# Second-layer attention of a three-layer model: probabilities divided by their sums before the transpose, values as the stationary operand

## The reference, cut to what matters

```python
qkv = h @ w_qkv + b_qkv                      # 3 x 16 heads x 64
q = qkv[0] * (NA_HEAD_DIM ** -0.5)
s = einsum('bhqd,bhkd->bhqk', qr, kb) + bias  # bias from rpb, 256 x 256 per head
s = where(key_mask, s, -inf)
a = softmax(s, axis=-1)
o = einsum('bhqk,bhkd->bhqd', a, vb)
return o @ w_o                               # (256 x 1024) @ (1024 x 1024)
```

## Time and profile before

| what | value |
|---|---|
| runs | 1015.31 us median of 3 (1015.08 to 1017.59) |
| profiled execution | 1015.26 us, span 1013.4 us |
| mean granted TensorE clock | 0.997 |
| TensorE busy | 993.4 us, 98% of the span, 5869 matmul records |
| VectorE, ScalarE, GpSimd busy | 635.6 (63%), 506.4 (50%), 129.3 us (13%) |
| chain that ended last | TensorE 91%, VectorE 5%, ScalarE 2% |
| mean DMA rate | 172 GB/s |

### The profile page before, as it was taken

The page is one execution under the profiler, slowest core; times in us unless marked ns, Lnnn a source line. Parts: engine busy times, 40 slices in busy tenths (PEclk is TensorE's granted clock), DMA queues, the critical chain, the costliest instruction groups (busy, mean ns, idle before and its releaser), DMA issues.

```text
span 1013.4 us, 14604 instructions
## 1 busy us (share of the span) xinstructions
PE 993.4 (98%) x5869; PEld 865.7 (85%) x5869; DVE 635.6 (63%) x981; ACT 506.4 (50%) x751; POOL 129.3 (13%) x207
## 2 busy tenths in 40 slices
PE   7999999999999999999999999999999999999997
PEld 6889788888888898988888888888989889999995
DVE  6867677555556875555765555568665877555554
ACT  7666745444444655554544444456564355434442
POOL 5000796800000000000000000012500000000000
PEclk9999999999999999999999999999999999999999
DMA  9944469955555564243475555545643337656521
GB/s 277 299 136 143 104 154 209 301 175 199 179 195 177 176 204 145 111 126 125 150 244 178 195 181 193 183 132 195 191 163 110 100 125 253 204 168 205 171 81 42
DMA packets 112724, 174.77 MB, mean 172 GB/s; under 512 B 5977, under 2 KB 73569, under 8 KB 112657
## 3 DMA queue, kind: packets, MB, share of 16 engines
q1 hardware_dynamic: 106224, 165.43, 51.0%
q0 software_dynamic: 6272, 8.15, 3.3%
q10 hardware_dynamic: 160, 0.27, 0.1%
HBM read 172.77 MB, written 1.05 MB: 172 GB/s over the span
## 4 chain that ended last, share of the span: by engine, by line
PE 91%; DVE 5%; ACT 2%; DMA 1%; issue 1%; SPq 0%; DVEq 0%; ACTq 0%
PE bank L1017 27%; PE bank L1019 27%; PE bank L1018 27%; PE bank L1130 2%; DVE wl L1531 1%; PE bank L1160 1%; PE bank L1032 1%; PE bank L1187 1%; DMA raw<-in_da_w_qkv_dram 1%; PE bank L1246 1%; PE bank L1193 1%; PE bank L1180 1%; PE bank L1140 1%; ACT wh L607 1%; PE bank L1163 0%
## 5 line engine op out<-in xcount | busy, mean ns | idle before, releaser
L1531 DVE TENSOR_TENSOR wl<-raw,wh 128x2048 fp32r<-128x2048 f32 x154 | 355.2, 2312 | 185.2 <-ACT wh L607 185.1
L607 ACT ACTIVATE wh<-raw 128x2048 fp32r<-128x2048 f32 x154 | 292.0, 1909 | 118.4 <-PE bank L1019 111.8
L1017 PE MATMUL bank<-wh,xh 128*128 128x512 f32 (+2 forms) x664 | 250.5, 377 | 1.6 <-DVE xl L1608 1.0
L1019 PE MATMUL bank<-wh,xl 128*128 128x512 f32 (+2 forms) x664 | 245.9, 370 | 0.0
L1018 PE MATMUL bank<-wl,xh 128*128 128x512 f32 (+2 forms) x664 | 245.8, 370 | 0.0
L1017 PE MATMUL bank<-xh,wh 128*128 128x256 f32 (+1 forms) x672 | 194.7, 290 | 1.0 <-DVE wl L1847 0.5
L1018 PE MATMUL bank<-xl,wh 128*128 128x256 f32 (+1 forms) x672 | 190.4, 283 | 0.0
L1019 PE MATMUL bank<-xh,wl 128*128 128x256 f32 (+1 forms) x672 | 190.4, 283 | 0.0
L1017 PEld LDWEIGHTS bank<-wh,xh 128*128 128x128 f32 (+1 forms) x664 | 125.2, 189 | 22.6 <-issue 2.0
L1019 PEld LDWEIGHTS bank<-wh,xl 128*128 128x128 f32 (+1 forms) x664 | 125.0, 188 | 22.2
L1018 PEld LDWEIGHTS bank<-wl,xh 128*128 128x128 f32 (+1 forms) x664 | 125.3, 189 | 20.3
(11 more groups left out here) (248 smaller groups left out, 854.4 us busy)
## 6 DMA issues: line engine op xcount, KB each, us to landing
raw<-in_w_ff_dram SPq DMA_DIRECT2D x32, 1024.0 KB, 5.2
raw<-in_ffn_w_gate_dram SPq DMA_DIRECT2D x44, 512.0 KB, 4.0
raw<-in_ffn_w_up_dram SPq DMA_DIRECT2D x44, 512.0 KB, 5.0
raw<-in_ffn_w_down_dram SPq DMA_DIRECT2D x22, 1024.0 KB, 5.0
raw<-in_na_w_qkv_dram SPq DMA_DIRECT2D x12, 1024.0 KB, 5.2
raw<-in_w_in_dram SPq DMA_DIRECT2D x12, 1024.0 KB, 5.2
raw<-in_da_w_qkv_dram SPq DMA_DIRECT2D x11, 1024.0 KB, 11.5
raw<-in_ple_w_gate_dram SPq DMA_DIRECT2D x8, 1024.0 KB, 5.0
```

Of the source, the lines that this page charges most:

```text
L607: nc.scalar.activation(wh[:, i % RING, :], raw[:, i % RAW, :], ACT.Copy).then_inc(s_hi, 1)
L1017: nc.tensor.matmul(dst, lh, rh, start=start, stop=False, skip_group_check=True)
L1019: return nc.tensor.matmul(dst, ll, rh, start=False, stop=stop, skip_group_check=True)
L1531: nc.vector.tensor_tensor(wl[:, i % RING, :], raw[:, i % RAW, :], wh[:, i % RING, :].bitcast(F32), ALU.subtract).then_inc(s_lo, 1)
```

## The change

In the second layer only. VectorE gets `norm(i)`: it divides the probabilities of item i by their sums, at step i+1, behind the shift. The transposes wait for `mixed` (by `norm`) in place of the exponentials. The value product takes 128 columns of values (both heads of the pair) as stationary and moves 128 columns of probabilities of one head, so the bank holds features on the partitions; of the 128 rows of each product only the 64 of its own head are used. ScalarE copies those rows per group of two items, two 64x256 copies, into a buffer in `hn` (`hold_values`), as `xh` is still in use by the quarters. In the tail `held_hi` and `held_lo` bring groups 0 to 5 to `xh` and `xl` in three 128x512 steps, and `values_hi` and `values_lo` bring groups 6 and 7 straight from banks 7 and 4. The head turns and `values_out` of this layer go. FILLS becomes 4, 4 and 4. The diff, cut to its core:

```diff
@@ -399,7 +400,7 @@
         TAIL = 14
-        FILLS = ({15: 4, 17: 2}, {15: 4, 16: 3, 17: 3})
+        FILLS = ({15: 4, 17: 2}, {15: 4, 16: 4, 17: 4})
         KEPT = (3, 4)
@@ -407,7 +408,17 @@
             return bank[(PARTS.index((part, c)) + 1) % 4]
-        GROUP = (4, 4, 8)
+        GROUP = (4, 2, 8)
+        o_turned = hn[:, :, :].rearrange("p b n -> p (b n)").rearrange("p (g s) -> p g s", g=8)
+        O_GROUPS = ((0, 2), (2, 4), (4, 6))
+        O_KEYS = (("att1", 0, 0), ("att1", 1, 0), ("att1", 0, 1))
+
+        def held(g0, g1):
+            at = (g0 + 4) % 8
+            return o_turned[:, at:at + g1 - g0, :]
+
+        def value_bank(i):
+            return bank[4] if i >= 14 else bank[7]
         STEPS_2 = [[], [0], [1, 2]] + [[s] for s in range(3, 19)] + [[]] * 8
@@ -728,6 +739,32 @@
                     value_squares(e // 4)
+                if l == 1 and e >= 0 and e % 2 == 1:
+                    hold_values(e // 2)
+
+            def values_of(g, half):
+                return value_bank(2 * g)[head_rows(half), :].rearrange("p (b m q) -> p b m q", b=TB, m=2)[:, :, half, :]
+
+            def hold_values(g):
+                wait(act, valued, 1, 2 * g + 1)
+                for half in range(2):
+                    dst = held(g, g + 1)[head_rows(half), 0, :].rearrange("p (b q) -> p b q", b=TB)
+                    ins = nc.scalar.activation(dst, values_of(g, half), ACT.Copy)
+                ins.then_inc(o_out1.sem, 1)
+
+            def held_hi(n):
+                g0, g1 = O_GROUPS[n]
+                if n == 0:
+                    used(act, first["v", 1, 3])
+                wait(act, o_out1, 1, g1 - 1)
+                nc.scalar.activation(xh[:, g0:g1, X0:XP], held(g0, g1), ACT.Copy).then_inc(turned_hi.sem, 1)
+
+            def values_hi(g):
+                wait(act, valued, 1, 2 * g + 1)
+                for half in range(2):
+                    dst = xh[head_rows(half), g, X0:XP].rearrange("p (b q) -> p b q", b=TB)
+                    ins = nc.scalar.activation(dst, values_of(g, half), ACT.Copy)
+                ins.then_inc(turned_hi.sem, 1)
@@ -774,14 +811,18 @@
                 copy_turned(1, 12)
+                hold_values(5)
                 exponentials(1, 14)
-                turn_hi("att1", 0, 0)
+                held_hi(0)
                 copy_turned(1, 13)
                 exponentials(1, 15)
-                turn_hi("att1", 1, 0)
+                held_hi(1)
                 copy_turned(1, 14)
+                held_hi(2)
+                copy_turned(1, 15)
+                values_hi(6)
+                values_hi(7)
                 split_to(first["wo", 1] + 4)
-                copy_turned(1, 15)
@@ -1047,8 +1089,10 @@
                     if name and b < TB:
-                        need(name, b, kh)
+                        need(name, 1 if (name, kh) == ("att1", 0) else b if name != "att1" else 0, kh)
                     for k in range(4):
+                        if (name, kh, b) == ("att1", 1, 0) and k >= 2:
+                            need(name, k - 1, kh)
                         ins = three(banks[b][0:c.stop - c.start, :], x_of(4 * kh + k, c), (w_hi[:, k, :], w_lo[:, k, :]),
@@ -1146,8 +1190,8 @@
                     b = i % 2
-                    if l == 0:
-                        wait(pe, mixed, 0, i)
+                    if l < 2:
+                        wait(pe, mixed, l, i)
                     else:
@@ -1170,8 +1214,8 @@
                         wait(pe, v_ready, 2, 2)
-                    if i % GROUP[l] == 0 and i:
-                        wait(pe, o_out0 if l == 0 else o_out, l, i // GROUP[l] - 1)
+                    if i % GROUP[l] == 0 and i and (l, i) != (1, 14):
+                        wait(pe, (o_out0, o_out1, o_out)[l], l, i // GROUP[l] - 1)
                     if (l, i) == (0, 15):
@@ -1181,11 +1225,10 @@
                         for m in range(2):
-                            hd = 2 * g + m
-                            dst = bank[7][:, 256 * b + 64 * (hd % 4):256 * b + 64 * (hd % 4) + 64]
+                            dst = value_bank(i)[:, 256 * b + P * m:256 * b + P * m + P]
                             for kb in range(2):
-                                ins = nc.tensor.matmul(dst, pt[:, b, 256 * m + P * kb:256 * m + P * kb + P],
-                                                       v_s[:, kb, 64 * hd:64 * hd + 64],
+                                ins = nc.tensor.matmul(dst, v_s[:, kb, P * g:P * g + P],
+                                                       pt[:, b, 256 * m + P * kb:256 * m + P * kb + P],
                                                        start=(kb == 0), stop=(kb == 1))
@@ -1395,7 +1435,8 @@
                     next(wo_first)
-                head_turns(1)
+                if l == 0:
+                    head_turns(1)
                 run(wo_first)
@@ -1657,8 +1698,10 @@
                     mix(s - 1)
+                if l == 1 and 0 <= s - 1 < 16:
+                    norm(s - 1)
                 e = s - 3
-                if l > 0 and 0 <= e < 16 and e % GROUP[l] == GROUP[l] - 1:
+                if l > 1 and 0 <= e < 16 and e % GROUP[l] == GROUP[l] - 1:
                     values_out(l, e // GROUP[l])
@@ -1692,6 +1735,32 @@
+            def norm(i):
+                g, b = i // 2, i % 2
+                wait(dve, exped, 1, i)
+                r_ = row_inv[:, b, 2 * g:2 * g + 2]
+                link(nc.vector.reciprocal(r_, row_sum[:, b, 2 * g:2 * g + 2]))
+                for m in range(2):
+                    at = slice(256 * m, 256 * m + 256)
+                    ins = nc.vector.tensor_scalar(prob[:, i % 3, at], prob[:, i % 3, at], r_[:, m:m + 1], None, ALU.mult)
+                ins.then_inc(mixed.sem, 1)
+
+            def held_lo(n):
+                g0, g1 = O_GROUPS[n]
+                wait(dve, turned_hi, *O_KEYS[n])
+                nc.vector.tensor_tensor(xl[:, g0:g1, X0:XP], held(g0, g1), xh[:, g0:g1, X0:XP].bitcast(F32),
+                                        ALU.subtract).then_inc(turned_lo.sem, 1)
+
+            def values_lo(g):
+                wait(dve, turned_hi, "att1", g - 5, 1)
+                for half in range(2):
+                    rows = head_rows(half)
+                    at = (rows, g, slice(X0, XP))
+                    src = value_bank(2 * g)[rows, :].rearrange("p (b m q) -> p b m q", b=TB, m=2)[:, :, half, :]
+                    ins = nc.vector.tensor_tensor(xl[at].rearrange("p (b q) -> p b q", b=TB), src,
+                                                  xh[at].bitcast(F32).rearrange("p (b q) -> p b q", b=TB), ALU.subtract)
+                ins.then_inc(turned_lo.sem, 1)
+
             def values_out(l, g):
@@ -1715,12 +1784,16 @@
                 shift(1, 14)
-                values_out(1, 2)
+                norm(13)
                 shift(1, 15)
-                turn_lo("att1", 0, 0)
-                turn_lo("att1", 1, 0)
+                held_lo(0)
+                norm(14)
+                held_lo(1)
+                norm(15)
+                held_lo(2)
+                values_lo(6)
+                values_lo(7)
                 split_to(first["wo", 1] + 4)
-                values_out(1, 3)
...
```

More of the change, by code:

```diff
@@ L238, in two_blocks_kernel @@
             TURNS += [(f"mix{l}", *k) for k in CB] + ([("meta", 0, 0)] if l == 0 else [])
-            TURNS += [(f"att{l}", b, c) for c in range(2) for b in range(2)]
+            TURNS += [(f"att{l}", b, c) for c in range(2) for b in range(2)] + ([("att1", 2, 1)] if l == 1 else [])
             TURNS += [(f"ffn{l}", *k) for k in CB]
@@ L264, in two_blocks_kernel @@
         rooted = Order(sem("rooted"), [(n,) for n in LATER if n != "mix1"])
-        turned = Order(sem("turned"), [k for k in TURNS if (k[0], k[2]) != ("att2", 1)])
+        turned = Order(sem("turned"), [k for k in TURNS if (k[0], k[2]) != ("att2", 1) and k[0] != "att1"])
         HALVED = [k for k in TURNS if (k[0], k[2]) != ("mix0", 0)]
@@ L282, in two_blocks_kernel @@
         exped = Order(sem("exped"), ATT)
-        mixed = Order(sem("mixed"), [(0, i) for i in range(16)])
+        mixed = Order(sem("mixed"), [(l, i) for l in range(2) for i in range(16)])
         p_turned = Order(sem("p_turned"), ATT)
@@ L287, in two_blocks_kernel @@
         o_out0 = Order(sem("o_out0"), [(0, 0), (0, 1), (0, 2), (0, 3, 0), (0, 3, 1)])
-        o_out = Order(sem("o_out"), [(1, g) for g in range(4)] + [(2, g) for g in range(2)])
+        o_out1 = Order(sem("o_out1"), [(1, g) for g in range(6)])
+        o_out = Order(sem("o_out"), [(2, g) for g in range(2)])
         head_sq = Order(sem("head_sq"), [(0, 0), (0, 1), (0, 2), (0, 3), (2, 0), (2, 1)])
@@ L889, in _ @@
                     head_norms(1, 0)
-                turns_hi(f"att{l}", 1)
+                if l == 0:
+                    turns_hi("att0", 1)
                 split_to(first["wo", l] + 2 + 4)
@@ L1363, in head_turns @@
                     for b in range(TB):
[L1364 to L1368, removed]
```

(6 more changed lines are left out.)

## The result

The changed kernel takes 1019.54 us (median of 6 runs, 1018.15 to 1020.46) against 1015.14 us for the kernel before (6 runs): ratio 1.0040, 95% interval 1.0027 to 1.0053. The profiled execution took 1019.97 us, with a span of 1018.2 against 1013.4. It is slower by 4.4 us, 0.4%; the interval begins a little under the 0.3% that was called the limit of the measurement.

A forecast was written before the change was run, and what follows sets the result against it. TensorE was taken to bound the slots, and engines waiting for each other the tail. +2.2 (late wo) - 0.8 (second turn) + 0.7 (backlog) = +2.1 us on 1015.26: forecast 1017.4, own range 1016.3 to 1018.3, stated range 1014.4 to 1019.3.

The forecast's parts named there:

- a clock of 0.50 near 457: Sign listed under wrong: TensorE's granted clock at half rate at the wo matmuls right after the pause.
- the late start of wo: In the tail, the wo unit starts at 457.0, 2.2 us late, including the first turn's 0.97 us.
- the clock rival: Wo matmuls after the pause at 457 run at half clock and lose 1.7 us: 1019.1 us, chance 0.17.
- Value products: nothing: Moving 128 columns in the 64 value products costs 0 us, bounds 0 and +1.
- Turns: -1.8: Sixteen head-turn transposes leave a full TensorE, in two groups worth 0.97 and 0.79 us.
- The division hidden in the slots: VectorE's normalising, about 0.8 us per step, costs 0 in the slots, covered by its idle time.
- The wait for bank 6: In the tail, transpose 12 waits for ScalarE's copy out of bank 6: 0.6 us of new idle time.
- The pause ahead of wo: TensorE pauses 3.2 us, against 0.46 before, for ScalarE's second held copy and VectorE's low half.
- The split backlog: Weight splits delay the residual additions to 478.3; TensorE stands about 0.7 us at the next norm's transposes, bounds 0 and +1.4.
- I take no fall: The clock stays up after the 3.2 us pause ahead of wo, as dense 512-column matmuls follow directly.

The follow-up runs named there:

- experiment 5: Changed kernel with the first two held copies ahead of exponentials 13 and the fourth wo unit's split moved earlier: 1013.83 us, 0.9987 of the kernel before.
- experiment 4: Kernel before with only the division moved ahead of the transpose; turns and 64-column products stay: 1015.76 us, ratio 1.0007 to the kernel before.
- Experiment 6: Changed kernel with early held copies, early fourth wo split, and ScalarE's copy 11 ahead of exponentials 13: 1013.22 us, 0.9983 of the kernel before.
- experiment 1: Changed kernel with the first two held copies ahead of exponentials 13 on ScalarE, low halves moved on VectorE: 1015.19 us, 0.9998 of the kernel before.
- experiment 3: Changed kernel with the fourth wo unit's split ahead of copy 14 on ScalarE and held low half 2 on VectorE: 1019.28 us, 1.0037 of the kernel before.
- experiments 2: Changed kernel with twelve unused 512-column matmuls filling the pause between value product 12 and the first wo matmul: 1017.67 us, 1.0025 of the kernel before.
- experiment 7: Changed kernel where the first two wo pieces wait only for groups 0 and 1, the third for 2 and 3: 1017.08 us, 1.0023 of the kernel before.

## Why the prediction was right, and which step failed

The median lies 0.24 us above the upper end of the range, while the interval of the ratio reaches into it (its lower end, 1.0027, is 1017.9 us). The forecast itself was 2.1 us too low. The prediction gave 0.79 to a time between 1012.3 and 1018.4 us and 0.18 to a slower one; the slower one came, with a sign that it had listed under "wrong", a clock of 0.50 near 457. It had the places and the waits right, it failed in one step, the clock, and it had one term, the late start of wo, too small. That the result lies so near the 1019.1 of the clock rival is partly luck: the rival's fall was priced 0.2 too high, and the late start that it shared with the forecast 0.9 too low.

- **Value products: nothing.** Right. A block of eight with 128 columns lasts 1.06 us where it lasted 1.00, but the next matmul follows after 0.81 to 0.82 us, as it did after 0.81. From score 0 to score 13 the change adds 0.07 us. The new form of the products was not run by itself; these spacings are the evidence.
- **Turns: -1.8.** Right in size; the second turn was then lost in the second pause, which experiment 5 took away.
- **The division hidden in the slots.** Right; experiment 4 shows it alone. The room was overstated: 31.35 us of idle VectorE over the 14 steps of the earlier trace rows is 2.2 us for a step, not 3, and it was still enough.
- **The wait for bank 6.** Predicted 0.6, measured 0.60, ended by the copy that was named. Experiment 6 removed it.
- **The pause ahead of wo.** Predicted 3.2 us, from ScalarE's list and VectorE's low half behind it; measured 3.31, with the first piece 3.06 us late where 2.2 was said. The mechanism held (experiment 1), the size was short. 0.2 of the difference is older, from the start and the slots. The rest are handovers that the walk counted too short: transpose 12 started at 450.90 and not at 450.45, 0.2 us of it beyond what is older; the held pair began 1.10 us after value product 11 and lasted 0.77, not 1.00 and 0.7, the exponentials and copies overlapped less, and 0.15 lay between the low half and the first matmul.
- **The split backlog.** Predicted 0.7, measured 0.67 of idle time and 0.95 in all, since the split transposes cost a second start. It was ended by hn, as written. The additions began at 480.91, not at 478.3, and TensorE reached the transposes 2.2 us later than said as well; both hang on the start of wo and on the clock, so the difference held. (By the prediction's own numbers, 481.05 less 480.45, it was 0.6.)
- **The clock: the step that failed.** "I take no fall" was wrong, and the rival with 0.17 is what came: predicted 1.7 us, measured 1.48 in the first four pieces. The reason given, dense matmuls right behind the pause, carried no weight: the clock was already low when the first of them ran (457.64 against 457.85). What the clock answered to lay ahead of that matmul. The trace before had one pause with a fall and one without, of the same length; a pause nearly twice as long should have made the fall the likelier case. The Trainium skill's page "TensorE: Matmul & The Clock Gate" (Parts 1 and 4) spoke for the fall, and the traces after and of experiment 3 agree with it on the fall; whether transposes count for less, no run here tells apart.

With the sizes measured: 3.06 late at wo, 1.48 of slow matmuls, less the 0.95 that the second turn (0.79) and the other order of wo pieces and steps (the remaining 0.16, not tested alone) save behind it, 0.26 of waiting for the first normed half (23.05 us in experiment 1 against 22.79 in 5 for the middle row of the table), and 0.95 for the second pause make 4.80, the difference of the spans.

## What to carry to other kernels

When a change takes work from the bounding engine and gives it to engines with room, look at the one place where their cover ends, and walk each engine's written order there, operation by operation; the average room says nothing of it. Work whose inputs have long been ready (the first two held copies) belongs ahead of the chain, not between its links, and long weight splits must not be queued behind the last result if something short stands behind them. And a pause of TensorE is to be priced with the slow matmuls that can follow it: here 3.3 us of idle time brought 1.5 us more.

## What the runs showed of the hardware

The clock doesn't answer to a pause in the same way each time. All nine kernels have the same pause of 1.82 to 1.86 us near 29 us, with eight 16-column transposes behind it. Six of the nine traces show the clock at 0.50 after it, that of before from 31.9 to 35.3; three do not, those of experiments 2, 3 and 5. This is experiment 5:

```profile
28.00:31.00 3.00, 1.15 (x11) 0.94 (x9) 2.72 (x13) 2.96 (x5) 0.61 (x2) 1.00 1.12 325
31.00:34.40 3.40, 3.40 (x32) 3.37 (x33) 2.85 (x2) 3.40 (x7) 0.00 (x0) 1.00 1.05 384
```

And the long pause of 3.3 us brought 3.4 us of low clock in one trace and 6.8 in another (experiment 3). Two pauses of 1.20 and 0.40 with six matmuls between them brought none (experiment 7). The six executions with the early fall start score 0 at 377.40 to 377.55 us, the three without it at 376.51, 376.75 and 377.25.

That part of the spread of a kernel's runs is which of its pauses the clock answered to is likely and not shown run by run. Of the 24 runs of the kernel before beside experiments 5 to 7, the six with a mean clock of 0.998 or 0.999 took 1013.88 to 1015.19 us, the seven at 0.995 or 0.996 took 1015.13 to 1016.76; this mean also counts a fall behind the last matmul, which every trace shows and which slows no matmul. Which property of a pause decides was not tried further and stays open.
